# Moving the common first instructions of two programs ahead of the branch that chooses between them

## The chip, the cores and the metric

The kernel runs on the 8 cores of one Trainium2 chip. Each core has five engines with their own instruction streams: PE (TensorE, matrix products), DVE (VectorE), ACT (ScalarE), POOL (GpSimd) and SP (SyncE, here only a queue that starts transfers). Transfers between HBM and the on-chip memory (SBUF) are started by ACT, POOL and SP and carried out by the core's 16 DMA engines. There is no traffic between cores. The metric is the device time of the slowest core in microseconds (us).

## What is computed

One layer of a streaming encoder, on 4 new streams of 4096 frames and on 32 running streams of 64 frames:

```
hn = rms_norm(x, norm1_g)
g_b, g_c, x_a, x_l, g_l = split(hn @ w_in)          # 1024 -> 2560 columns
out_a = g_b * conv3_causal(g_c * x_a)               # mixer A, 512 channels
out_b = rg_lru(conv4_causal(x_l) + b) * gelu(g_l)   # mixer B, a recurrence in time
x = x + concat([out_a, out_b]) @ w_out
x = x + square(relu(rms_norm(x, norm2_g) @ w_up)) @ w_down    # 1024 -> 4096 -> 1024
y = rms_norm(x, norm_f_g)
```

Outputs are y for both groups of streams and the new states of the two convolutions and of the recurrence.

## The kernel before

Two cores share a new stream. The even core does its first 2304 frames, the odd core the remaining 1792. The recurrence runs over the whole stream, so the odd core first recomputes, for the frames of its neighbour, what the state of the recurrence needs (tiles named L). Every core also does 4 running streams (256 rows, tile S). Even cores therefore run the chain of tiles S, M0, M1, M2, M3, M4, and odd cores L0, S, L1 to L4, M0 to M3. An M tile has 512 or 384 rows, an L tile 512 or 256.

The two chains are two programs in one binary. `arm(False)` and `arm(True)` record, for each engine, a list of instructions with their semaphore waits; `emit` (L148) writes both. On every engine the emitted code first reads the word `side` from HBM into a register (L162, two instructions of the form TENSOR_LOAD), then branches (L163): value 0 runs the first program, which stands right behind the branch, and otherwise the second, which stands behind the whole of the first (`make`, L159). Everything else, the first transfer included, stands behind this branch.

What happens first in either program is the work of four strands, generators that yield one instruction at a time:

- `g_par` loads the parameters `par` through ACT's queue and derives small constants in `sb_der` on DVE and ACT;
- `g_xloads` loads rows of x into the 8 slots of 128x1024 f32 (512 KB each) of `sb_xsl`, through ACT's queue. For S and M tiles one transfer fills one slot (`xs` and `xp`); for L tiles, whose input `xl` is stored transposed, one transfer fills two slots (1 MB);
- `g_setup` clears or sets small tiles on POOL (`sb_identb`, ones in `sb_gfb`, `sb_cst`, `sb_halx`, `sb_halp`, `sb_h_p`);
- `g_conv` starts the casting transfers of the weights through POOL's queue: 512 KB of f32 in HBM (`wall`, one chunk of 84) become 256 KB of bf16. The 20 chunks of `w_in` land in SBUF (`sb_ring`, then `sb_uT`), used from there by S, the L tiles and M0, and are written back to `wscr` in HBM through SP (`g_back`) for the later tiles. The other 64 chunks go from HBM to HBM, and SP loads them from `wscr` into a ring when they are needed. `wbd` (the gates' weights) and `wout` are cast by POOL too.

`Weaver` sets the order. It keeps an estimated clock for each engine and each path of transfers, and always emits the waiting instruction with the earliest estimated start. So the position of an instruction in its engine's stream depends on the estimates of all that was emitted before it, and an engine runs its stream in that order, whatever is ready.

PE needs for the first tile: rows in `sb_xsl`, their squares on ACT (`sb_junk`), a scaled copy on DVE (`sb_hb`), transposes on PE (L697), the gain on DVE (into `sb_hT` or, for M0 of the even cores, `sb_uS`), and then the projections with the cast chunks (L776; with the ring, L780). L855 are the gates, L989 is the output projection, L1037 and L1087 are the MLP.

## Time and profile before

| | |
|---|---|
| runs shown | 998.66 us median of 3 (908.91 to 1062.85) |
| profiled execution | 909.05 us, span of its slowest core 907.5 us |
| spans, even cores 0, 2, 4, 6 | 904.6, 903.0, 905.1, 907.5 us |
| spans, odd cores 1, 3, 5, 7 | 901.6, 901.8, 899.8, 902.1 us |
| PE busy on core 6 | 839.3 us (92%) |
| DVE, ACT, POOL busy on core 6 | 425.2, 376.3, 184.9 us |
| moved by core 6 | 158.26 MB |

All times in the profile count from the first instruction of the core in question. "Busy" is the time in which an engine executed something. A row of the timeline gives start, duration, engine, line, operation and names; an engine's name with a q behind it is its instruction sequencer, which is where transfers are started and registers loaded.

### The profile page before, as it was taken

To read this page: it belongs to the slowest core of one execution; us is meant where nothing else is said; L and a number is where in the kernel's file an instruction comes from. 1 tells how busy PE (TensorE), PEld (TensorE's weight loads), DVE (VectorE), ACT (ScalarE), POOL (GpSimd) and SP (SyncE) were. 2 spreads that over 40 slices of the span, in tenths; PEclk is the share of its full clock that TensorE was granted. 3 is DMA by queue.
4 is the path that set the end of the run, shared out by engine and by line. 5 is a ranking of instruction groups with operands and counts; after the bars stand their busy time and mean duration, and the time that the engine had idled before them with its cause. 6 is when DMAs were issued, how large, how long until landed. Compare 5 with 4: busy or idle time off the path is not lost.

```text
span 907.5 us, 15041 instructions; the slowest of 8 cores (899.8 to 907.5 us)
## 1 busy us (share of the span) xinstructions
PE 839.3 (92%) x4392; PEld 428.5 (47%) x4464; DVE 425.2 (47%) x722; ACT 376.3 (41%) x754; POOL 184.9 (20%) x307
## 2 busy tenths in 40 slices
PE   2679789699999999999999999999999899999995
PEld 2444345255564444444444444555445455446542
DVE  4698886663301210636665434575315477514112
ACT  4578738552331000554942134583205485205301
POOL 4132240234453000232100013120003212003200
PEclk9799889899999999999999999999999999999998
DMA  8999999999888534685553369565248852778751
GB/s 237 205 180 215 214 117 130 134 180 177 163 182 168 145 96 126 241 318 172 141 149 84 117 164 300 163 166 161 84 151 254 267 159 73 233 198 271 206 163 73
DMA packets 80441, 158.26 MB, mean 174 GB/s; under 512 B 9184, under 2 KB 9312, under 8 KB 80352
## 3 DMA queue, kind: packets, MB, share of 16 engines
q1 hardware_dynamic: 61632, 111.76, 42.4%
q0 software_dynamic: 15264, 33.30, 23.2%
q10 hardware_dynamic: 3456, 12.14, 4.1%
q8 instruction: 40, 0.66, 0.3%
q14 instruction: 49, 0.40, 0.2%
HBM read 165.75 MB, written 32.57 MB: 219 GB/s over the span
## 4 chain that ended last, share of the span: by engine, by line
PE 82%; DMA 8%; DVE 4%; issue 3%; ACT 2%; POOL 0%; POOLq 0%; DVEq 0%; ACTq 0%; SPq 0%
PE ps L1037 28%; PE ps L1087 27%; PE ps L780 12%; PE ps L989 7%; DMA sb_ring<-wscr 4%; PE ps L776 3%; DMA sb_uT<-wall 3%; PE ps L1079 2%; PE ps L697 1%; PE ps L1097 1%; DMA sb_xsl<-xp 1%; PE ps L855 1%; ACT sb_t_rig L532 1%; PE ps L1074 1%; DVE sb_t_xc L882 1%
## 5 line engine op out<-in xcount | busy, mean ns | idle before, releaser
L1037 PE MATMUL ps<-sb_hT,sb_ring 128*128 128x512 bf16 (+2 forms) x1050 | 194.3, 341 | 6.2 <-DVE sb_a_pb L535 4.3
L532 ACT ACTIVATE sb_junk<-sb_xsl 128x1024 bf16<-128x1024 f32 (+1 forms) x59 | 59.6, 1010 | 269.7 <-DVE sb_xsl L535 256.6
L535 POOL TENSOR_TENSOR sb_uT<-sb_rl 128x512 bf16<-128x512 bf16 (+1 forms) x80 | 83.0, 1038 | 418.4 <-ACT sb_stat L532 272.7
L532 ACT ACTIVATE sb_rl<-ps 128x512 bf16<-128x512 f32 (+2 forms) x192 | 98.1, 525 | 142.2 <-PE ps L1037 127.8
L1037 PEld LDWEIGHTS ps<-sb_hT,sb_ring 128*128 128x128 bf16 x1064 | 104.4, 99 | 91.3 <-issue 8.4
L535 DVE TENSOR_TENSOR sb_xsl<-ps,sb_xsl 128x512 f32<-128x512 f32 (+1 forms) x60 | 46.1, 794 | 200.7 <-PE ps L1087 139.9
L1087 PE MATMUL ps<-sb_ring,sb_uT 128*128 128x512 bf16 x576 | 138.5, 379 | 0.8
L1087 PE MATMUL ps<-sb_uS,sb_uT 128*128 128x512 bf16 x423 | 95.7, 379 | 0.5
L1037 PE MATMUL ps<-sb_hT,sb_uS 128*128 128x512 bf16 (+1 forms) x466 | 92.6, 354 | 0.3
L1087 PEld LDWEIGHTS ps<-sb_ring,sb_uT 128*128 128x128 bf16 x592 | 57.6, 98 | 67.8
L780 PE MATMUL ps<-sb_hT,sb_ring 128*128 128x512 bf16 (+1 forms) x369 | 81.8, 367 | 5.0 <-DMA sb_ring<-wscr 4.6
L535 DVE TENSOR_TENSOR sb_uT<-sb_rl 128x512 bf16<-128x512 bf16 (+1 forms) x80 | 34.0, 425 | 102.6 <-ACT sb_rl L532 90.3
L989 PE MATMUL ps<-sb_wout,sb_mix 128*128 128x512 bf16 x314 | 71.2, 379 | 0.3
L1037 PEld LDWEIGHTS ps<-sb_hT,sb_uS 128*128 128x128 bf16 x472 | 46.0, 98 | 42.9
L1087 PEld LDWEIGHTS ps<-sb_uS,sb_uT 128*128 128x128 bf16 x432 | 42.1, 98 | 49.0 <-issue 0.2
L780 PEld LDWEIGHTS ps<-sb_hT,sb_ring 128*128 128x128 bf16 x376 | 37.1, 99 | 43.4 <-issue 8.4
L532 ACT ACTIVATE sb_t_rig<-sb_t_rig 128x512 f32<-128x512 f32 (+4 forms) x72 | 48.3, 680 | 20.6 <-DVE sb_t_rig L543 19.9
L535 DVE TENSOR_TENSOR sb_hT<-ps,sb_par 128x1024 bf16<-128x1024 bf16 x36 | 43.8, 1220 | 24.7 <-PE ps L697 24.5
L780 PE MATMUL ps<-sb_hT,sb_uS 128*128 128x384 bf16 (+1 forms) x262 | 53.1, 347 | 0.6 <-DVE sb_t_xb L548 0.5
L543 DVE SCALAR_TENSOR_TENSOR sb_t_xc<-sb_t_xb,sb_par,sb_t_xc 128x512 f32<-128x512 f32 (+2 forms) x72 | 46.4, 657 | 13.3 <-ACT sb_t_xc L532 12.1
L532 ACT ACTIVATE sb_t_rig<-sb_t_rig,sb_cst 128x1536 f32<-128x1536 f32 (+5 forms) x48 | 48.2, 1009 | 2.1 <-POOL sb_t_rig L551 0.3
L989 PEld LDWEIGHTS ps<-sb_wout,sb_mix 128*128 128x128 bf16 x320 | 31.2, 98 | 37.5 <-issue 0.7
(100 smaller groups left out, 841.7 us busy)
## 6 DMA issues: line engine op xcount, KB each, us to landing
sb_ring<-wscr SPq DMA_DIRECT2D x240, 256.0 KB, 3.5
sb_uS<-wscr SPq DMA_DIRECT2D x160, 256.0 KB, 3.0
wscr<-wall POOLq DMA_DIRECT2D x64, 256.0 KB, 10.8
sb_xsl<-xp ACTq DMA_DIRECT2D x18, 512.0 KB, 8.7
yp<-sb_xsl POOLq DMA_DIRECT2D x13, 512.0 KB, 7.9
sb_uT<-wall POOLq DMA_DIRECT2D x16, 256.0 KB, 24.1
wscr<-sb_uT SPq DMA_DIRECT2D x16, 256.0 KB, 14.4
sb_wout<-wout POOLq DMA_DIRECT2D x4, 512.0 KB, 13.1
```

Of the source, the lines that this page charges most:

```text
L532: return OP("act", dur, lambda e: e.activation(out=out, in_=in_, func=func, **kw), rd_, wr_)
L535: return OP(eng, dur, lambda e: e.tensor_tensor(out=out, in0=in0, in1=in1, op=op), rd_, wr_)
L543: return OP("dve", dur, lambda e: e.scalar_tensor_tensor(out=out, in0=in0, scalar=scalar, in1=in1, op0=op0, op1=op1), rd_, wr_)
L697: yield PE(0.55, [lambda e, kc=kc: e.transpose(out=pb[:, kc * 128:(kc + 1) * 128], in_=hb_ap[:, kc * 128:(kc + 1) * 128], identity=identb[ ...
L776: lambda e, kc=kc: e.matmul(out=bank_ap(b, N), lhsT=ap[:, kc * 128:(kc + 1) * 128], rhs=h_ap(t, False, kc, col0, N), start=(kc == 0), stop ...
L780: lambda e, kc=kc: e.matmul(out=bank_ap(b, N), lhsT=slot[:, kc * 128:(kc + 1) * 128], rhs=h_ap(t, False, kc, col0, N), start=(kc == 0), st ...
L855: yield PE(0.25, [lambda e, gi=gi, b=b: e.matmul(out=bank_ap(b, N), lhsT=wbd[:, (gi * 4 + c) * 128:(gi * 4 + c + 1) * 128], rhs=T["xcb"][: ...
L882: yield OP("dve", 1.35, lambda e: e.tensor_tensor_scan(out=h, data0=a, data1=i_, initial=h0_p[:, c:c + 1], op0=ALU.mult, op1=ALU.add), [T[ ...
L989: yield PE(4 * 0.217, [lambda e, kc=kc, half=half, b=b, j=j: e.matmul(out=bank_ap(b), lhsT=mix[:, kc * 512 + j * 128:kc * 512 + (j + 1) * ...
L1037: return lambda slot: [lambda e, kc=kc: e.matmul(out=bank_ap(b, q.N), lhsT=slot[:, kc * 128:(kc + 1) * 128], rhs=h_ap(q, True, kc, 0, q.N) ...
L1079: yield PE(32 * 0.217, [lambda e, kc=kc, j=j, bs=bs: e.matmul(out=bank_ap(bs[j]), lhsT=u_ap(t, kc, j * 128, 128), rhs=held[kc // 2][:, (kc ...
L1087: lambda e, i=i, q=q, j=j, b=b: e.matmul(out=bank_ap(b), lhsT=u_ap(q, 2 * kp + i, j * 128, 128), rhs=slot[:, i * 512:(i + 1) * 512], start ...
```

## The change

The inputs are laid out anew on the host: a new array `head` of 128 x 6144 f32 (3 MB) holds what six slots of `sb_xsl` hold at the start, for even cores the two blocks of S and the four of M0, for odd cores the first 2 MB of L0 and the two blocks of S. The array `xs` is gone. The strand `g_head` loads it in four transfers (2, 2, 1 and 1 slots) and fixes which slots belong to which tile; `g_xloads` goes on with the third tile of the chain.

`Weaver.lead` emits a given number of instructions of a strand at once, without choosing by the clock. Each arm first emits: 1 of `g_par` (the transfer of `par`), 4 of `g_head`, 4 of `g_conv` (the casts of chunks 12 to 15), 8 of `g_setup` and 1 more of `g_conv` (the cast of `wbd`). These are the same instructions in both arms, so `emit` writes them once, ahead of the register load and the branch; `cut` is how many each engine has (5 on ACT, 13 on POOL, none on PE, DVE and SP). The rest of each program follows as before, with the order found by the clock from that state on. What is computed does not change.

```
-def emit(nc, arms, side):
+def emit(nc, arms, cut, side):
...
     def make(name):
         def f(e):
+            n = cut[name]
+            put(e, arms[0].prog[name][:n])
             r = e.alloc_register("side")
             e.reg_load(r, side[0:1, 0:1])
             with e.If_eq(r, 0):
-                put(e, name, arms[0])
+                put(e, arms[0].prog[name][n:])
             with e.Else():
-                put(e, name, arms[1])
+                put(e, arms[1].prog[name][n:])
...
+    def lead(self, gen, n):
+
+        s, val = Strand(gen, -99, 0), None
+        pace, self.PACE = self.PACE, {}
+        while n:
+            s.req, val = gen.send(val), None
+            if s.req[0] == "get":
+                val = s.req[1].take(s.req[2])
+            else:
+                self._emit(s, self._start(s.req))
+                n -= 1
+        self.PACE = pace
...
-        Ss = mk_tile("S", "S", xs, 0, 256, 4, 1.5, ys, 0)
+        Ss = mk_tile("S", "S", head, 0, 256, 4, 1.5, ys, 0)
...
+        def g_head():
+            for k, n in ((0, 2), (2, 2), (4, 1), (5, 1)):
+                yield DMA("act", xsl[:, k * D:(k + n) * D], head[:, k * D:(k + n) * D], [], [xsl_b[k + i] for i in range(n)], "x", 0.52 * n)
+            for k in range(6):
+                P_x.free.remove(k)
+            if second_half:
+                Ls[0].xs, Ss.xs = {0: [0, 1], 1: [2, 3]}, {0: 4, 1: 5}
+            else:
+                Ss.xs, Ms[0].xs = {0: 0, 1: 1}, {0: 2, 1: 3, 2: 4, 3: 5}
+            for t in chain[:2]:
+                for _ in t.xs:
+                    W.mark("x" + t.name)
+
         def g_xloads():
-            for t in chain:
+            for t in chain[2:]:
...
-        W.spawn(g_setup(), -20)
-        W.spawn(g_conv(order), 500)
-        W.spawn(g_par(), -19)
-        W.spawn(g_xloads(), -10)
+        setup, conv, pars, rows = g_setup(), g_conv(order), g_par(), g_head()
+        for gen, n in ((pars, 1), (rows, 4), (conv, 4), (setup, 8), (conv, 1)):
+            W.lead(gen, n)
+        cut = {e: len(S.prog[e]) for e in S.ENG}
+        for gen, prio in ((setup, -20), (conv, 500), (pars, -19), (rows, -11), (g_xloads(), -10)):
+            W.spawn(gen, prio)
...
+    tall = lambda a: a.reshape(-1, 128, D).transpose(1, 0, 2).reshape(128, -1)
...
-            "xs": f(x_sample[4 * c:4 * c + 4].reshape(256, D)),
+            "head": f(np.concatenate([wide[:, :4096], few] if hf else [few, tall(rows[:512])], axis=1)),
```

How the streams stand now is shown at three places, all in the program of the even cores or ahead of the branch. In the changed file the lines of the helpers have moved down by 16 (L532 is L548, L551 is L567) and those of the mixer by 30 (L776 is L806); L162 and L163 are L165 and L166.

The start of ACT's stream, before:

```order
L171 UNCONDITIONAL_BRANCH
L162 TENSOR_LOAD side_ptr
L162 TENSOR_LOAD side
L163 COMPARE_AND_BRANCH
L112 DMA sb_par<-par 128x156
L112 DMA sb_xsl<-xs 128x1024 x2
L112 DMA sb_xsl<-xp 128x1024 x6
L532 ACTIVATE sb_der<-sb_der 128x4 x3
L112 DMA sb_gfb<-gf 128x1024
L532 ACTIVATE sb_junk,sb_stat<-sb_xsl 128x1024
```

and in the changed kernel:

```order
L174 UNCONDITIONAL_BRANCH
L112 DMA sb_par<-par 128x156
L112 DMA sb_xsl<-head 128x2048 x2
L112 DMA sb_xsl<-head 128x1024 x2
L165 TENSOR_LOAD side_ptr
L165 TENSOR_LOAD side
L166 COMPARE_AND_BRANCH
L112 DMA sb_xsl<-xp 128x1024 x2
L548 ACTIVATE sb_der<-sb_der 128x4 x3
L112 DMA sb_gfb<-gf 128x1024
L548 ACTIVATE sb_junk,sb_stat<-sb_xsl 128x1024
```

Five transfers (78 KB and 3 MB) stand ahead of the register load; the two behind it are the first of M1.

The start of POOL's stream, before:

```order
L162 TENSOR_LOAD side_ptr
L162 TENSOR_LOAD side
L163 COMPARE_AND_BRANCH
L551 MEMSET sb_identb 128x128
L112 DMA sb_ring<-wall 128x1024
L588 AFFINE_SELECT sb_identb<-sb_identb 128x128
L551 MEMSET sb_gfb 128x128
L551 MEMSET sb_cst 128x1
L112 DMA sb_ring<-wall 128x1024
L551 MEMSET sb_cst 128x1
L551 MEMSET sb_halx 128x12
L551 MEMSET sb_halp 128x8
```

and in the changed kernel:

```order
L112 DMA sb_ring<-wall 128x1024 x4
L567 MEMSET sb_identb 128x128
L604 AFFINE_SELECT sb_identb<-sb_identb 128x128
L567 MEMSET sb_gfb 128x128
L567 MEMSET sb_cst 128x1 x2
L567 MEMSET sb_halx 128x12
L567 MEMSET sb_halp 128x8
L567 MEMSET sb_h_p 128x4
L112 DMA sb_wbd<-wbd 128x1024
L165 TENSOR_LOAD side_ptr
L165 TENSOR_LOAD side
L166 COMPARE_AND_BRANCH
```

The four casts of chunks 12 to 15 are first of all, the cast of `wbd` follows the eight small instructions, and the casts into `sb_uT` come right behind the branch.

PE's first work in the program of the even cores, before:

```order
L697 MATMUL ps<-sb_identb,sb_hb 128x128 x24
L776 MATMUL ps<-sb_hT,sb_ring 128x256 x24
L697 MATMUL ps<-sb_identb,sb_hb 128x128 x16
L776 MATMUL ps<-sb_hT,sb_uT 128x256 x24
L855 MATMUL ps<-sb_t_xcb,sb_wbd 128x256 x4
L776 MATMUL ps<-sb_hT,sb_uT 128x256 x8
L855 MATMUL ps<-sb_t_xcb,sb_wbd 128x256 x2
```

and in the changed kernel:

```order
L727 MATMUL ps<-sb_identb,sb_hb 128x128 x24
L806 MATMUL ps<-sb_hT,sb_ring 128x256 x24
L806 MATMUL ps<-sb_hT,sb_uT 128x256 x8
L727 MATMUL ps<-sb_identb,sb_hb 128x128 x16
L806 MATMUL ps<-sb_hT,sb_uT 128x256 x16
L885 MATMUL ps<-sb_t_xcb,sb_wbd 128x256
L806 MATMUL ps<-sb_hT,sb_uT 128x256 x8
```

One projection of S with the first chunk in `sb_uT` (8 products) now stands ahead of two transposed blocks of M0, and one pair of gates is split. Such exchanges go on through the even program's first three tiles and through the whole L part of the odd one.

## Rows read from the trace of the kernel before

**Rows 1.** Spans and mean TensorE clock of the cores.

```profile
core 0: 904.6 us, clock 0.979
...
core 5: 899.8 us, clock 0.950
core 6: 907.5 us, clock 0.976
core 7: 902.1 us, clock 0.946
```

**Rows 2.** Busy time of each engine by stretch, core 6.

```profile
core 6: us, PE busy (x) PEld busy (x) DVE busy (x) ACT busy (x) POOL busy (x), PEclk, DMA share, GB/s
20.00:60.00 40.00, 25.82 (x185) 18.51 (x185) 29.31 (x71) 24.82 (x61) 9.84 (x23) 0.84 1.04 200
60.00:180.00 120.00, 99.47 (x501) 48.78 (x509) 92.33 (x163) 80.57 (x138) 30.77 (x60) 0.91 0.99 164
180.00:300.00 120.00, 118.90 (x655) 64.47 (x667) 38.01 (x59) 39.49 (x82) 49.57 (x77) 1.00 0.94 178
```

**Rows 3.** Chain that ended last, core 6: start, duration, what.

```profile
1.02 0.90 POOLq L162
1.95 0.52 POOLq L162
...
7.64 26.93 DMA sb_uT<-wall
...
144.09 13.34 DMA sb_ring<-wscr
```

**Rows 4.** Timeline of core 6, start of ACT, POOL and PE.

```profile
2.58 0.38 ACTq L112 DMA_DIRECT2D sb_par<-par  x1
3.16 0.72 POOL L112 DMA_DIRECT2D sb_ring<-wall  x1 [0.34 <-POOL sb_identb L551]
3.95 3.94 ACTq L112 DMA_DIRECT2D sb_xsl<-xp  x6
6.60 3.20 POOL L112 DMA_DIRECT2D sb_uT<-wall  x6
10.69 1.06 ACT L532 ACTIVATE sb_junk<-sb_xsl 128x1024 bf16<-128x1024 f32 x1 [0.30 <-POOL sb_a_pb L548]
30.44 1.87 PE L776 MATMUL ps<-sb_hT,sb_uT 128*128 128x256 bf16 x8 [4.91 <-DMA sb_uT<-wall]
```

**Rows 5.** Transfers of core 6: KB each, median us from issue to landing.

```profile
sb_xsl<-xs ACTq DMA_DIRECT2D x1, 512.0 KB, 4.3
sb_xsl<-xs ACTq DMA_DIRECT2D x2, 512.0 KB, 5.4
```

**Rows 6.** Timeline of core 7, start of POOL, ACT and DVE.

```profile
5.50 0.20 POOL L551 MEMSET sb_identb<- 128x128 bf16 x1 [4.79 <-issue]
9.44 0.72 POOL L112 DMA_DIRECT2D sb_ring<-wall  x1 [3.73 <-issue]
9.94 1.11 ACTq L112 DMA_DIRECT2D sb_xsl<-xl  x2
20.38 2.28 DVE L539 TENSOR_SCALAR sb_hT<-sb_xsl,sb_par 128x512 bf16<-128x512 f32 x4 [1.49 <-DMA sb_xsl<-xl]
```

**Rows 7.** Queue: packets, MB, engine share; core 6, 8 to 12 and 20 to 24 us.

```profile
q10 hardware_dynamic: 234, 0.83, 54.8%
q0 software_dynamic: 222, 0.39, 51.8%
...
q0 software_dynamic: 171, 0.32, 51.4%
q10 hardware_dynamic: 175, 0.65, 51.2%
```

**Rows 8.** Transfers of core 7 from 10 to 12 us, then 12 to 16 us.

```profile
DMA packets 30, 0.02 MB, mean 9 GB/s; under 512 B 0, under 2 KB 30, under 8 KB 30
...
DMA packets 321, 0.83 MB, mean 208 GB/s; under 512 B 32, under 2 KB 130, under 8 KB 259
```

More of the change, by code:

```diff
@@ L143, in check_no_deadlock, with put @@
             raise RuntimeError("static deadlock: " + "; ".join(msg))
-def emit(nc, arms, side):
-    def put(e, name, S):
-        for waits, fns, inc in S.prog[name]:
+def emit(nc, arms, cut, side):
+    def put(e, part):
+        sem = arms[0].sem
+        for waits, fns, inc in part:
             for k, v in waits:
-                e.wait_ge(S.sem[k], v)
+                e.wait_ge(sem[k], v)
             ins = None
@@ L156, in put @@
             if inc is not None:
-                ins.then_inc(S.sem[inc[0]], inc[1])
+                ins.then_inc(sem[inc[0]], inc[1])
     def make(name):
         def f(e):
+            n = cut[name]
+            put(e, arms[0].prog[name][:n])
             r = e.alloc_register("side")
@@ L381, in dout @@
         return nc.dram_tensor(name, list(shape), dt, kind="ExternalOutput").ap()
-    xp, xl, xs = din("xp", [NF, D]), din("xl", [128, 8 * NF]), din("xs", [256, D])
+    xp, xl, head = din("xp", [NF, D]), din("xl", [128, 8 * NF]), din("head", [128, 6 * D])
     side_d = din("side", [1, 1], mybir.dt.int32)
@@ L645, in arm @@
         chain = Ls[0:1] + [Ss] + Ls[1:] + Ms
+        assert [t.J if not t.lean else 4 for t in chain[:2]] in ([4, 2], [2, 4])
         def xap(k):
@@ L1188, in arm @@
         S.check_no_deadlock()
-        return S, W
+        return S, W, cut
     with es:
         arms = [arm(False), arm(True)]
-        emit(nc, [a[0] for a in arms], side_d)
+        emit(nc, [a[0] for a in arms], arms[0][2], side_d)
+        assert arms[0][2] == arms[1][2]
     return nc, arms[0][1], arms[1][1]
@@ L1225 @@
         rows[:len(mine)] = mine
+        wide = f(np.concatenate([x_prompt[s, a:a + n].reshape(n, 8, 128).transpose(2, 1, 0).reshape(128, 8 * n)
+                                 for a, n in zip(np.cumsum((0,) + SKIP), SKIP)], axis=1))
+        few = tall(x_sample[4 * c:4 * c + 4].reshape(256, D))
         st = np.concatenate([sca[4 * c:4 * c + 4].reshape(8, 512), slc[4 * c:4 * c + 4].reshape(12, 512), slh[4 * c:4 * c + 4]], axis=0)
@@ L1230 @@
             "xp": rows,
-            "xl": f(np.concatenate([x_prompt[s, a:a + n].reshape(n, 8, 128).transpose(2, 1, 0).reshape(128, 8 * n)
-                                    for a, n in zip(np.cumsum((0,) + SKIP), SKIP)], axis=1)),
-            "xs": f(x_sample[4 * c:4 * c + 4].reshape(256, D)),
+            "xl": wide,
+            "head": f(np.concatenate([wide[:, :4096], few] if hf else [few, tall(rows[:512])], axis=1)),
             "side": np.full((1, 1), hf, np.int32),
```

## Prediction

> **What bounds the kernel now.** I read the spans first. The metric is the slowest core, and that is an even core: core 6 ends at 907.5 us, core 0 at 904.6; the odd cores shown end at 899.8 and 902.1 [rows 1]. A gain on odd cores alone is worth nothing, and a loss there costs nothing before it exceeds 907.5 - 902.1 = 5.4 us. The profiled execution took 909.05 us, 1.5 more than its longest span; my sum is made against it. The median of the three runs shown, 998.66, is far above it and their lowest, 908.91, is beside it; I forecast the time of an execution like the profiled one.
>
> Next, the busy times by stretch on core 6 [rows 2]. From 180 to 300 us PE is busy 118.90 of 120: from there on the end is fixed by PE's own work. From 20 to 60 it is busy 25.82 of 40 and from 60 to 180 99.47 of 120, while the DMA engines' share is 1.04 and 0.99. So the core is short of transfers there, and what the change does to the end is how much earlier or later the stream of transfers, and PE behind it, gets through the first 180 us.
>
> The chain agrees [rows 3]: after two register loads (1.02 to 2.47 us) and a few starts on POOL it is 26.93 us of a casting transfer into `sb_uT`; much later a load of the ring (13.34 us from 144.09) is in it. PE's first wait for such a cast ends at 30.44, after 4.91 us of idling [rows 4]. Not ACT, not DVE, but bytes in a full pipe decide when the S tile gets on.
>
> **The start of the even cores.** ACT issues its first transfer at 2.58 and POOL its first cast at 3.16, behind the 1.5 us of register loads and branch [rows 3, 4]. With nothing ahead of them both can go at about 1.05, where the first load now starts: 1.5 us earlier on ACT, 2.1 on POOL. Both feed the same 16 engines, so I take 1.8.
>
> What stands behind must not fall dry. ACT: 0.4 for `par`, two transfers of two slots at 0.55 each (a pair took 1.11 on core 7 [rows 6]), two of one slot at up to 0.66 (3.94 for six [rows 4]), which ends at about 3.9; loads and branch 1.5, to 5.4; the two transfers of M1 1.3, to 6.7. Before, the last of the eight was issued at 3.95 + 3.94 = 7.9, so ACT's arithmetic can start 1.2 earlier. POOL: four casts (0.72, then 0.53 each, from 3.20 for six [rows 4]) to 3.4, the eight small instructions beside and behind them, `wbd` to about 4.2, loads and branch to 5.7, and the first cast into `sb_uT` there instead of at 6.60. These casts queue: in the chain one takes over 26 us from issue to landing, so the 0.9 matters as little as the 1.5 us of branch that now sits between the two groups. Price of a dry queue: those 1.5 us once; the 5.5 MB issued ahead cover it (below).
>
> On even cores the first transfer now brings both blocks of S. Before, they were issued right behind `par`, at about 3.0 and 3.5; block 0 took 4.3 to land and the median of the two is 5.4, so block 1 took 6.5: they landed at 7.3 and 10.0 [rows 5]; ACT squared the first from 10.69 on [rows 4], held by the derivation of the constants. Now both land together near 10.0 - 1.5 = 8.5, ACT is ready at about 9.5. So the coarser transfer costs nothing; without that cover it would be 10.0 - 7.3 = 2.7 us on the first square, and still ahead of the 4.91 us that PE waits for a cast.
>
> **The neighbour.** This is the term that decides. Core 7 has to run the second program, and issues its first cast at 9.44 and its first rows at 9.94 [rows 6]. From 10 to 12 us it moves 9 GB/s, from 12 to 16 208 GB/s [rows 8]. So before 12 us core 6 streams alone. What is that worth? In 8 to 12 us core 6 served 234 packets of ACT's queue in 54.8% of 16 x 4 us, 0.150 us each, and 222 of POOL's in 51.8%, 0.149 each. In 20 to 24 us, with core 7 streaming, 175 took 51.2%, 0.187 each, and 171 took 51.4%, 0.192 each [rows 7]. Packets have the same mean size (3.5 to 3.7 KB, 1.8 to 1.9 KB). With the neighbour, a packet takes 1.27 times as long.
>
> After the change the odd cores start at the same time as the even ones, since the shared head needs no branch. The 8.4 us of lone streaming (3.6 to 12 us) are gone: the same packets take 8.4 x 0.27 = 2.3 us longer. From 12 to 20 us the neighbour was still coming up; if half of the rise was missing there, another 0.7 at most. So the even cores lose 2.3 to 3.0 and gain 1.8: +0.5 to +1.2 us, of which I take +0.8. Bounds: if the dearer packet has another cause (later packets differ, SP's write-backs), the loss is 0 and the sum -1.8; if all of 12 to 20 us was cheap too, it is 16.4 x 0.27 = 4.4, and the sum +2.6.
>
> The Trainium skill, HBM Reference, Specifications, says that the two cores of a domain share its bandwidth, each getting about 358 GB/s with both streaming. By that a core at 305 GB/s (core 6 from 8 to 12 us: 1.22 MB in 4 us) would lose nothing to its neighbour, and the time would come out at the -1.8 of the first rival; core 6's own packets speak against it here.
>
> **The odd cores.** First rows at about 1.5 instead of 9.94: 8.4 us earlier, so the first cast into `sb_hT` (20.38 [rows 6]) could come at 12. At most that takes core 7 from 902.1 to 893.7; the new L orders may eat some. It does not show in the metric.
>
> **The new order.** It moves no work. One projection of S with a chunk of `sb_uT` now stands ahead of 16 transposes of M0, which will wait for that chunk; M0's products come long after, so I cost it at nothing. If such an exchange goes wrong where nothing covers it, the nearest row is PE's wait for one cast, 4.91 us [rows 4]; exchanged luckily it may give as much. PE's idle time in 60 to 180 us, 20.5 us [rows 2], is what can be won at all.
>
> **Sum.** 909.05 - 1.8 + 2.6 = 909.8 us.
>
> **Rivals.**
> Rival 1, the neighbour costs nothing. For: HBM may not be the reason of the dearer packet. Against: all of it falls together with core 7's start. Then 909.05 - 1.8 = 907.3 us.
> Rival 2, the order wins: an exchange takes away one wait like the 4.91. For: PE has 20.5 us of idle time there. Against: nothing says which way it goes. 909.8 - 4.9 = 904.9 us.
> Rival 3, slower: an exchange puts PE behind a cast or a DVE result that it did not wait for, with later work queued behind it. Same price, 909.8 + 4.9 = 914.7 us; it decides once the blocked work is needed before 60 us, where PE still idles a third of the time.
> Rival 4, slower by code. The odd cores' second program is not at hand after the branch: POOL idles 4.79 us until 5.50 and 3.73 more until 9.44 [rows 6], with nothing else in flight. Now 3 MB of rows and 2.5 MB of weights are queued; at the 0.97 MB in 4 us of the later pair in rows 7 they fill 22 us. If the code comes behind all of it, core 7 starts at 22 + 6.9 (9.44 - 2.55) + about 2 = 31 instead of 20.38, ends at 912.7, and the run is 914.2 us. It decides when that first cast comes after 20.38 + 5.4 = 25.8. Against: code has a queue of its own. The Trainium skill, Runtime: NRT & Kernel Launch, Instruction fetch mechanics, says that a taken branch out of the window forces a transfer of the target page first; the trace agrees with the two idle times, and the page says nothing of what data does to them.
>
> **How the numbers follow.** Forecast, 909.8 (own range 907.5 to 912.5): 0.45. Rival 1: 0.2. Rival 2: 0.15. Rival 3: 0.12. Rival 4: 0.08. The range takes in rivals 1 and 2 with 0.3% of scatter (2.7 us) below rival 2 and as much above rival 3: 902 to 917.5. Only several such exchanges, or a fetch that waits twice, leave the 2% (18 us) that a measurement of this kernel tells from no change: slower 0.04, faster 0.03, same 0.93.
>
> **What the profile of the changed kernel would show.** First issues of ACT and POOL at about 1.05 on all cores; first branch on ACT ending near 5.4, on POOL near 5.7. Core 6's packets at 0.19 rather than 0.15 us in 8 to 12 us, and no more than 250 GB/s there. PE's first wait for a cast ending between 29 and 32. Core 7's first cast into `sb_hT` near 12 and its span under 900. Even cores still the slowest, within 3 us of before. Packets at 0.15 us and core 6 near 905.7 would speak for rival 1, a core 7 above core 6 for rival 4, equal transfers with another PE idle time in 60 to 180 us for rivals 2 and 3.

## The result and the profile after

The changed kernel takes 912.28 us in the median (910.63 to 915.83) where the one before takes 910.31; the ratio is 1.0032, 95% interval 1.0024 to 1.0041, so +2.9 us. The forecast was +0.8. Four of the 19 executions before ran 10 to 17% longer at a lower clock on some cores; such executions are left out of every ratio and mean below, and the median of the other 15 is 909.51. The profiled execution of the changed kernel took 914.98 us, 2.7 above its median, and the one before 909.05, 0.5 below 909.51: so the two traces differ by more than the kernels do (5.9 us against 2.9), and the readings below show the kind of loss and not its exact size. These are its spans and clocks; beside [rows 1], the even cores are later and the odd ones earlier:

```profile
core 0: 910.4 us, clock 0.978
...
core 2: 913.4 us, clock 0.976
...
core 5: 898.5 us, clock 0.944
core 6: 910.1 us, clock 0.978
core 7: 900.8 us, clock 0.944
```

The mean over all its executions is 909.3 on the even cores and 898.1 on the odd ones; with the kernel before it was 904.1 to 906.1 and 899.5 to 902.1 on the five chips on which the experiments ran. The clocks are those of [rows 1] to within 0.006.

Where did the time arise? Start with the timeline of core 6, changed kernel, ACT, POOL and PE (start, duration; in brackets the engine's idle time ahead of the row), beside [rows 4]:

```profile
1.07 0.38 ACTq L112 DMA_DIRECT2D sb_par<-par  x1
1.59 2.33 POOL L112 DMA_DIRECT2D sb_ring<-wall  x4 [0.88 <-POOLq L391]
10.98 1.05 ACTq L112 DMA_DIRECT2D sb_xsl<-xp  x2
12.07 1.06 POOL L112 DMA_DIRECT2D sb_uT<-wall  x2 [6.06 <-issue]
14.80 1.06 ACT L548 ACTIVATE sb_junk<-sb_xsl 128x1024 bf16<-128x1024 f32 x1 [0.30 <-issue]
34.25 1.87 PE L806 MATMUL ps<-sb_hT,sb_uT 128*128 128x256 bf16 x8 [6.36 <-DMA sb_uT<-wall]
```

Both queues start 1.5 us earlier, as meant. Then nothing is issued from 3.8 to 10.98 on ACT. The next view, the instructions of the register load on core 6 (duration in ns, min/median/max, then the start in us), shows why:

```profile
L165 SPq TENSOR_LOAD <-side_ptr x1: 860/860/860, 1.1 to 1.1; - x1
...
L165 ACTq TENSOR_LOAD <-side_ptr x1: 5886/5886/5886, 3.8 to 3.8; - x1
L165 POOLq TENSOR_LOAD <-side_ptr x1: 5184/5184/5184, 5.4 to 5.4; - x1
L165 ACTq TENSOR_LOAD <-side x1: 1144/1144/1144, 9.7 to 9.7; - x1
L165 POOLq TENSOR_LOAD <-side x1: 844/844/844, 10.7 to 10.7; - x1
```

SP reads its word from HBM while nothing streams, in 0.86 us. ACT and POOL read theirs behind their own 3 MB and take 5.9 and 5.2 us for the first of the two loads; I had put 1.5 us for both loads and the branch. The first square comes 4.1 us later than before, the first cast into `sb_uT` 5.5. Core 6 is the mildest case: on cores 0, 2 and 4 ACT's two loads take 8.9, 7.9 and 8.3 us, and the first square comes 6.3 to 6.5 us later than before.

The transfers of core 6, by queue in 8 to 12 us, answer to [rows 7]:

```profile
DMA packets 202, 1.00 MB, mean 250 GB/s; under 512 B 10, under 2 KB 10, under 8 KB 103
...
q10 hardware_dynamic: 101, 0.81, 69.8%
q0 software_dynamic: 101, 0.19, 30.6%
```

ACT's packets are now twice as large (8 KB), so I compare by bytes: 0.81 MB in 69.8% of 16 x 4 us is 55 us per MB; before it was 0.83 MB in 54.8%, 42. That is 1.30 times, and 250 GB/s is the bound that the prediction named. POOL's packets have the size of before (1.8 to 1.9 KB) and take 0.194 us (30.6% of 64 us, 101 packets) instead of 0.149, as forecast. By stretch (columns as in [rows 2]), core 6, first before the change, then changed:

```profile
0.00:4.00 4.00, 0.00 (x0) 0.00 (x0) 0.00 (x0) 0.00 (x0) 1.23 (x7) 1.00 0.07 17
4.00:8.00 4.00, 0.00 (x0) 0.00 (x0) 0.79 (x4) 0.02 (x1) 4.00 (x14) 1.00 0.97 252
8.00:12.00 4.00, 0.00 (x0) 0.00 (x0) 1.19 (x6) 3.04 (x7) 3.89 (x11) 1.00 1.07 306
12.00:16.00 4.00, 1.16 (x10) 0.95 (x11) 2.14 (x5) 3.47 (x10) 0.00 (x0) 1.00 1.05 313
16.00:20.00 4.00, 2.61 (x20) 1.94 (x19) 3.79 (x5) 2.18 (x6) 0.00 (x0) 1.00 1.07 285
```

```profile
0.00:4.00 4.00, 0.00 (x0) 0.00 (x0) 0.00 (x1) 0.00 (x0) 2.62 (x9) 1.00 0.49 98
4.00:8.00 4.00, 0.00 (x0) 0.00 (x0) 0.79 (x4) 0.00 (x0) 1.38 (x9) 1.00 0.97 238
8.00:12.00 4.00, 0.00 (x0) 0.00 (x0) 0.00 (x0) 0.00 (x0) 0.00 (x0) 1.00 1.00 250
12.00:16.00 4.00, 0.00 (x0) 0.00 (x0) 1.04 (x7) 3.05 (x6) 3.93 (x11) 1.00 1.04 219
16.00:20.00 4.00, 1.36 (x14) 1.39 (x15) 2.11 (x5) 3.72 (x10) 1.34 (x3) 1.00 1.00 222
```

The last column times 4 us is the bytes. The earlier start brings 0.32 MB in the first 4 us; the next 16 us lose 0.91 MB, and in 12 to 20 us the loss per us is the largest. At 20 us core 6 has moved 4.11 instead of 4.69 MB; over the four even cores the mean is 3.98 instead of 4.75. At the 250 GB/s that both cores of a pair then get, 0.77 MB is 3.1 us. Part of that is made up at once: from 20 to 24 us core 6 runs at 321 GB/s, where it had 247. PE's wait for its first cast into `sb_uT` ends at 34.25 instead of 30.44 (34.50, 35.35 and 36.53 on cores 4, 2 and 0). The first product of the down projection starts at 282.1 on the mean of the even cores instead of 276.1 (278.4 in e_order and 277.7 in n_before, two kernels of the table below). From 180 to 300 us PE is busy for 120.00 of 120 us.

The chain on core 6 has the same kind of casting transfer as [rows 3], 7 us later:

```profile
14.68 29.71 DMA sb_uT<-wall
```

Core 7, beside [rows 6], starts at once and then stalls; its casts into `sb_uT` and its first write of L0 into `sb_hT` come late (the other odd cores write `sb_hT` from 23.96, 24.36 and 25.00):

```profile
1.48 3.26 ACTq L112 DMA_DIRECT2D sb_xsl<-head  x4
...
20.86 3.70 POOL L112 DMA_DIRECT2D sb_uT<-wall  x7 [14.86 <-issue]
...
26.19 4.65 DVE L555 TENSOR_SCALAR sb_hT<-sb_xsl,sb_par 128x512 bf16<-128x512 f32 x8
```

Where the 14.86 us of idling went is told by POOL's loads and branch on core 7, the branch of the kernel before first, then the changed kernel:

```profile
L163 POOLq COMPARE_BRANCH  x1: 45/45/45, 2.4 to 2.4; - x1
```

```profile
L165 POOLq TENSOR_LOAD <-side_ptr x1: 4440/4440/4440, 5.4 to 5.4; - x1
L165 POOLq TENSOR_LOAD <-side x1: 3994/3994/3994, 9.9 to 9.9; - x1
L166 POOLq COMPARE_BRANCH  x1: 45/45/45, 13.9 to 13.9; - x1
```

The two loads take 8.4 us. From the branch to POOL's first cast behind it are 7.0 us (13.9 to 20.86), and before the change they were 7.0 as well (2.4 to 9.44).

### The profile page after: what moved, and what is told of

Read it like the earlier page. It is cut to its first block, busy times and chain, and to the rows that moved or that the text cites. A ratio compares the mean times of both kernels' runs of the same rounds, so it can differ in the third digit from the quotient of the medians.

```text
span 913.4 us, 15044 instructions; the slowest of 8 cores (895.5 to 913.4 us)
## 1 busy us (share of the span) xinstructions
PE 839.4 (92%) x4392; PEld 429.8 (47%) x4464; DVE 426.6 (47%) x718; ACT 376.4 (41%) x754; POOL 182.1 (20%) x307
## 4 chain that ended last, share of the span: by engine, by line
PE 82%; DMA 7%; issue 4%; DVE 3%; ACT 2%; POOLq 1%; POOL 0%; DVEq 0%; ACTq 0%; SPq 0%
PE ps L1067 27%; PE ps L1117 27%; PE ps L810 12%; PE ps L1019 7%; PE ps L806 4%; DMA sb_ring<-wscr 4%; DMA sb_uT<-wall 2%; PE ps L727 2%; PE ps L1109 2%; PE ps L1127 1%; DMA sb_xsl<-xp 1%; PE ps L885 1%; PE ps L1104 1%; DVE sb_t_xc L559 1%; ACT sb_t_rig L548 1%
## 5 line engine op out<-in xcount | busy, mean ns | idle before, releaser
L1067 PE MATMUL ps<-sb_hT,sb_ring 128*128 128x512 bf16 (+2 forms) x1048 | 194.4, 340 | 10.3 <-DMA sb_ring<-wscr 8.7
L548 ACT ACTIVATE sb_junk<-sb_xsl 128x1024 bf16<-128x1024 f32 (+1 forms) x59 | 59.5, 1009 | 270.8 <-DVE sb_xsl L551 265.5
L551 POOL TENSOR_TENSOR sb_uT<-sb_rl 128x512 bf16<-128x512 bf16 (+1 forms) x80 | 81.5, 1018 | 414.4 <-ACT sb_stat L548 272.3
L548 ACT ACTIVATE sb_rl<-ps 128x512 bf16<-128x512 f32 (+2 forms) x192 | 97.8, 524 | 145.9 <-PE ps L1067 134.4
L551 DVE TENSOR_TENSOR sb_xsl<-ps,sb_xsl 128x512 f32<-128x512 f32 (+1 forms) x56 | 45.5, 839 | 200.8 <-PE ps L1117 140.7
L551 DVE TENSOR_TENSOR sb_uT<-sb_rl 128x512 bf16<-128x512 bf16 (+1 forms) x80 | 34.2, 428 | 102.2 <-ACT sb_rl L548 95.0
L551 DVE TENSOR_TENSOR sb_hT<-ps,sb_par 128x1024 bf16<-128x1024 bf16 x36 | 43.9, 1220 | 30.7 <-PE ps L727 30.3
L548 ACT ACTIVATE sb_t_rig<-sb_t_rig 128x512 f32<-128x512 f32 (+4 forms) x72 | 48.4, 680 | 12.5 <-DVE sb_t_rig L559 10.5
L727 PE MATMUL ps<-sb_identb,sb_hb 128*128 128x128 bf16 x320 | 27.6, 242 | 27.3 <-DVE sb_hb L555 24.9
L548 ACT ACTIVATE sb_t_rig<-sb_t_rig,sb_cst 128x1536 f32<-128x1536 f32 (+5 forms) x48 | 48.3, 1012 | 2.3 <-POOL sb_t_rig L567 0.3
## 6 DMA issues: line engine op xcount, KB each, us to landing
wscr<-wall POOLq DMA_DIRECT2D x64, 256.0 KB, 10.5
```

The lines of the kernel that those rows point to most:

```text
L548: return OP("act", dur, lambda e: e.activation(out=out, in_=in_, func=func, **kw), rd_, wr_)
L551: return OP(eng, dur, lambda e: e.tensor_tensor(out=out, in0=in0, in1=in1, op=op), rd_, wr_)
L727: yield PE(0.55, [lambda e, kc=kc: e.transpose(out=pb[:, kc * 128:(kc + 1) * 128], in_=hb_ap[:, kc * 128:(kc + 1) * 128], identity=identb[ ...
L1067: return lambda slot: [lambda e, kc=kc: e.matmul(out=bank_ap(b, q.N), lhsT=slot[:, kc * 128:(kc + 1) * 128], rhs=h_ap(q, True, kc, 0, q.N) ...
```

## Experiments

The table gives each kernel's ratio and, since the slowest core is nearly always an even one unless the odd ones are held back, the mean span of the even and of the odd cores over the executions of the ratio, less that of the kernel before on the same chip, with twice the standard error. The second column is the start in us of core 7's first transfer of rows in the profiled execution (9.9 in the kernel before; the other odd cores lie up to 4 us beside it, in e_odd_late7 7 to 10 us behind it).

| kernel | odd rows from | ratio, 95% | even, us | odd, us |
|---|---|---|---|---|
| n_before | 10.5 | 1.0010 (1.0000 to 1.0021) | +0.5 ± 0.6 | -0.1 ± 1.0 |
| b_place | 9.1 | 1.0014 (1.0001 to 1.0026) | +0.4 ± 0.6 | +0.1 ± 0.9 |
| e_head | 10.4 | 1.0018 (1.0009 to 1.0028) | +1.3 ± 0.5 | +1.7 ± 0.6 |
| e_head_rows | 9.8 | 1.0014 (0.9999 to 1.0030) | +1.0 ± 0.7 | +2.5 ± 0.7 |
| e_order | 9.8 | 1.0008 (1.0000 to 1.0017) | +0.8 ± 0.7 | -0.5 ± 1.2 |
| e_order_rows | 9.0 | 1.0030 (1.0019 to 1.0041) | +1.7 ± 0.5 | +3.1 ± 0.6 |
| e_oldorder | 1.5 | 1.0031 (1.0015 to 1.0048) | +2.3 ± 0.7 | -5.9 ± 1.6 |
| e_oldorder_rows | 1.5 | 1.0037 (1.0021 to 1.0052) | +3.1 ± 0.8 | +0.3 ± 1.2 |
| e_regfirst | 2.8 | 1.0039 (1.0022 to 1.0055) | +2.9 ± 0.9 | -11.2 ± 0.7 |
| e_old_regfirst | 2.8 | 1.0048 (1.0034 to 1.0062) | +3.8 ± 0.8 | -8.1 ± 0.9 |
| a_rows | 1.5 | 1.0029 (1.0017 to 1.0042) | +2.6 ± 0.5 | -0.4 ± 0.9 |
| e_odd_one | 4.4 | 1.0035 (1.0022 to 1.0047) | +3.2 ± 0.6 | -3.2 ± 1.1 |
| b_odd_one | 13.2 | 1.0003 (0.9993 to 1.0013) | 0.0 ± 0.6 | +1.2 ± 0.9 |
| e_odd_late2 | 16.9 | 1.0050 (1.0032 to 1.0067) | -1.1 ± 1.2 | +10.3 ± 0.9 |
| b_odd_two | 19.2 | 1.0027 (1.0015 to 1.0038) | -0.6 ± 1.1 | +5.9 ± 0.9 |
| e_pairs | 3.1 (core 5), 38.4 (core 7) | 1.0242 (1.0214 to 1.0270) | +3.1 ± 1.3 (0, 4), -0.5 ± 1.1 (2, 6) | -6.5 (1, 5), +27.8 (3, 7) |
| b_odd_late4 | 37.2 | 1.0169 (1.0147 to 1.0190) | -3.7 ± 1.0 | +20.9 ± 0.9 |
| e_odd_late7 | 36.6 | 1.0268 (1.0242 to 1.0294) | -1.4 ± 0.9 | +29.4 ± 1.1 |

### What the comparison itself shows for no change

n_before is the kernel before, unchanged.

> The kernel before itself, unchanged, run as if it were a changed kernel: what this comparison shows for no change. If the +0.8 to +1.7 us of the four kernels with `head` and nothing hoisted are a bias of the comparison, this shows it too: even cores about +1.2. If they belong to the kernels: even and odd cores within 0.5 us (twice the standard error of such a difference was 0.5 to 0.7), ratio 1.000.

It came out at 1.0010 and +0.5 us on the even cores. So differences of 0.5 us on the even cores, and 0.9 on the slowest, are not told from nothing here, and the changed kernel's 1.0032 may hold some 0.9 us of this. Everything below is read against that floor.

### Everything but the earlier start

e_order is the changed kernel with `n = 0` in `make`: the array, the large transfers and the new order are there, but nothing stands ahead of the branch.

> The changed kernel with nothing ahead of the branch: new array, new order of both programs, start as before. Theory A (the two register loads, which take 9 us behind the queued rows, are the cost): no loss is left, ratio to before 0.999 to 1.001, core 6 near 908. Theory B (the new order costs: SP has 15 write-backs instead of 10 ahead of the first load of the ring, PE waits for it): the loss stays, ratio 1.003 to 1.006, first product from the ring on even cores near 120 us instead of 109, first L1087-type product (down projection) 4 to 8 us later than before. Theory C (the neighbour's early traffic): odd cores start late again, so like A.

1.0008, +0.8 us on the even cores: most of the loss appears only when instructions are moved ahead of the branch (1.0032 - 1.0008 = 0.0024 or 2.2 us, each against the kernel before of its own set). PE's first projection starts at 17.8 us (19.3 before).

e_head has the old order and six transfers of 512 KB, but out of `head`:

```
-                    yield DMA("act", xap(k), t.src[t.row0 + j * 128:t.row0 + (j + 1) * 128, :], [], [xsl_b[k]], "x", 0.52)
+                    if t in chain[:2]:
+                        src = head[:, k * D:(k + 1) * D]
...
+                    yield DMA("act", xap(k), src, [], [xsl_b[k]], "x", 0.52)
```

> Edit: e_oldorder with nothing taken out of the branches, so the only difference from the kernel before is the array `head`, whose 128 rows are 24 KB apart where two rows of the old arrays were 4 KB apart. Theory 1 (the neighbour's early traffic is the whole loss): nothing starts earlier on any core, so even and odd cores stay within 0.5 us of the kernel before, ratio 1.000 (0.999 to 1.001). Rival (the array's spread rows cost time themselves, as a comparison of b_odd_late4's even cores, 901.3, with e_odd_late7's, 903.6, would allow): even cores 1 to 2 us later, ratio 1.001 to 1.002.

+1.3 us, which looked like a price of the layout. (Its odd cores also load L0's first 2 MB in four transfers of 512 KB instead of two of 1 MB; they are at +1.7.) Four further kernels tested that. In the three with `_rows` the array is `din("head", [6 * 128, D])`, read as `head[k * 128:(k + 1) * 128, :]`; b_place only makes `xs` 2 MB longer.

> Edit: e_head, with `head` stored as 768 rows of 4 KB, one behind the other, as the old arrays were, instead of 128 rows of 24 KB; same bytes, same transfers. Theory P (the 1.3 us that e_head's even cores lost come from the spread of the addresses: a tile's 128 rows lie 24 KB apart): even cores back within 0.4 us of before, ratio 1.000 (0.999 to 1.001), and core 0 moves 260 GB/s again in 4 to 8 us where e_head moved 227. Theory Q (another array at another place, whatever its shape, or chance): even cores 1 to 1.5 us later again, ratio 1.0015 to 1.002.

> Edit: e_order (new order and `head`, nothing taken out of the branches), with `head` stored as 768 rows of 4 KB. e_order was at +0.7 us on even cores, e_head (old order, `head`) at +1.3, so the new order by itself should be -0.6. Theory P: even cores 0.6 us (0 to 1) ahead of the kernel before, ratio 0.999 to 1.000. Theory Q: +0.7 as e_order, ratio 1.001.

> Edit: the changed kernel, with `head` stored as 768 rows of 4 KB; the transfers of two slots read two blocks of 128 such rows. Theory P: even cores 1.3 us earlier than in the changed kernel (+3.1 to +3.5 over before there), so at +1.8 to +2.2, ratio 1.002; what is left is the neighbour less the earlier start. Theory Q: as the changed kernel, 1.0032. Rival R (the neighbour alone is the whole loss and e_head's was chance): 1.003 or more, with e_head_rows at 1.000.

> The kernel before, with the array `xs` made 2 MB longer (it carries the first 512 rows of the prompt as well, which nothing reads from there), so that it has the size of `head` and shifts what lies behind it by the same 2 MB; every transfer reads the same rows in the same order as before. If the +1.2 us of the kernels with `head` come from where the arrays lie in memory: even cores +1 us, odd cores +1.5 to +2.5, ratio 1.001. If they come from reading the first prompt rows out of the same array as the samples, or from the doubled number of separate first transfers on the odd cores: within 0.5 us of before, ratio 1.000.

Theory P falls: with rows of 4 KB the even cores are at +1.0, +1.7 and, with the head hoisted, +2.6. The placement falls too (+0.4). What stays: the four kernels with `head` and nothing hoisted are at +0.8, +1.7, +1.3 and +1.0, 1.2 on the mean, where n_before and b_place are at +0.5 and +0.4. So some 0.7 ± 0.5 us come with `head` or the order of its transfers. Two kernels with late odd cores, on one chip and both in the old order, point the same way: e_odd_late7, with `head`, has its even cores at -1.4 ± 0.9, b_odd_late4, without it, at -3.7 ± 1.0. On what they rest stays open: neither the rows' distance nor the array's place, and no view of the traces shows a place for it (e_head_rows has moved as many bytes by 20 us as before: 239 against 241 GB/s on core 0, 234 against 235 on core 6). These kernels, not the one before, are the right zero for what follows.

### The earlier start and the neighbour, one by one

e_oldorder is e_head with the first 7 instructions of ACT and 13 of POOL ahead of the branch. e_old_regfirst is the same but reads the register before them, so that the even cores start when they did before, and only the odd ones earlier:

```
         def f(e):
             n = cut[name]
-            put(e, arms[0].prog[name][:n])
             r = e.alloc_register("side")
             e.reg_load(r, side[0:1, 0:1])
+            put(e, arms[0].prog[name][:n])
             with e.If_eq(r, 0):
```

> The order of before on every engine and in both programs, six transfers of 512 KB from the new array, and the common first part (7 instructions of ACT, 13 of POOL) ahead of register load and branch. Theory A: register loads again take about 9 us under traffic, ratio 1.003 or more. Theory B: no loss, ratio at or under 1.000, first product from the ring near 109 + what the start costs. Theory C: ratio 1.002 to 1.003 with packets of 0.19 us in 8 to 12 us.

> As e_oldorder, but the register loads come first and the common part behind them. Even cores then start at 2.5 as before, in the same order as before; only the odd cores' transfers start 7 us earlier. Theories A and B: ratio 1.000, odd cores 2 to 8 us shorter. Theory C: whatever loss there is beyond 1.000 is the neighbour's; my estimate was 2.3 to 3.0 us, ratio 1.0025 to 1.0033.

The even cores' own earlier start, with the slower register loads behind it, is worth 2.3 - 3.8 = -1.5 ± 1.1 us (same chip). The odd cores' start, 7 us earlier, costs +3.8 over before, and 3.8 - 1.3 = 2.5 ± 1.0 over e_head (two chips). Core 6 of e_old_regfirst, by stretch, against the five rows of before above:

```profile
4.00:8.00 4.00, 0.00 (x0) 0.00 (x0) 0.70 (x4) 0.00 (x0) 4.00 (x14) 1.00 1.00 163
8.00:12.00 4.00, 0.00 (x0) 0.00 (x0) 0.17 (x1) 1.80 (x4) 3.79 (x11) 1.00 1.02 207
12.00:16.00 4.00, 0.00 (x0) 0.00 (x0) 1.92 (x8) 2.96 (x8) 0.00 (x0) 1.00 1.07 221
16.00:20.00 4.00, 1.32 (x12) 1.11 (x13) 1.21 (x2) 1.53 (x4) 0.00 (x0) 1.00 0.99 251
```

POOL is as busy as before and the engines' share is full, but the bytes fall from 252, 306, 313 and 285 GB/s to these: by 1.55, 1.48, 1.42 and 1.14. That is 1.26 MB by 20 us, 5 us at 250 GB/s; about half of it, 2.5, reaches the end. Part is made up: on the mean of the even cores 1.26 MB are missing at 20 us and 0.95 at 60.

e_regfirst is the changed kernel with the register load put first in the same way.

> The changed kernel with the register loads first, then the common part, then the branch. The loads should take 0.9 and 0.5 us again, and the first transfers start at about 2.5 on all cores, on even cores as before. Theory A: the loss goes, ratio 0.999 to 1.001; first square on ACT near 10.7 instead of 14.8. Theory B: ratio 1.003 or more, whatever the start. Theory C (odd cores now stream from 2.5 us on): 1.002 to 1.003.

1.0039 against 1.0032 for the changed kernel, and 2.9 - 0.8 = +2.1 ± 1.1 us over e_order for the neighbour alone. With the loads in front again and the first square on core 6 at 10.87 the even cores are no faster. This kernel takes away two things together, the slow register loads (5.9 + 1.1 us) with the late square, and the 1.5 us of earlier start, so what is shown is that the two nearly balance; what either costs alone is not shown. The DMA engines did not fall dry meanwhile: in the changed kernel their share is 1.00 from 8 to 12 us, although nothing is started until 10.98. That is the prediction's cover (5.5 MB in the queues) at work, longer than I had asked of it. The odd cores gain 11 us: core 7 issues its casts into `sb_uT` from 14.68 instead of 20.86.

### One kernel, two pairs early and two late

In e_pairs (e_old_regfirst, with 14 further register loads on cores 3 and 7 ahead of the head) cores 0 and 4 have an early neighbour and cores 2 and 6 a late one, in the same executions.

```
+                r2 = e.alloc_register("idle")
+                with e.If_eq(r, 2):
+                    for _ in range(14):
+                        e.reg_load(r2, side[0:1, 0:1])
...
-            "side": np.full((1, 1), hf, np.int32),
+            "side": np.full((1, 1), 2 if c in (3, 7) else hf, np.int32),
```

> As e_old_regfirst (order of before, register loads first, common part behind them), but on cores 3 and 7 fourteen more register loads stand ahead of the common part and hold their transfers back by about 7 us; cores 1 and 5 start at 2.5. If the loss comes from the neighbour of the pair: cores 0 and 4 show packets of 0.20 to 0.30 us in 4 to 12 us and reach their down projection at 281 to 285 us as in e_old_regfirst, cores 2 and 6 show 0.15 us and reach it at 274 to 279 as before, and end 3 to 6 us ahead of 0 and 4. If it comes from all eight cores starting at once: the four even cores are alike and between the two.

```profile
core 0: 909.4 us, clock 0.975
...
core 2: 903.6 us, clock 0.980
...
core 4: 907.7 us, clock 0.979
...
core 6: 902.9 us, clock 0.979
```

Cores 0 and 4 are at +3.2 and +3.0 over the kernel before, cores 2 and 6 at -0.6 and -0.5 (means over executions). No floor of a comparison enters the 3.6 ± 1.7 us between the pairs. The same queues tell it; q10 and q0 in 8 to 12 us, first core 0, then core 2:

```profile
q10 hardware_dynamic: 169, 0.62, 59.9%
q0 software_dynamic: 144, 0.27, 42.6%
```

```profile
q10 hardware_dynamic: 234, 0.83, 55.1%
q0 software_dynamic: 219, 0.39, 51.7%
```

A packet of q10 takes 0.227 us (59.9% of 64 us, 169 packets) and one of q0 0.189 beside a streaming neighbour, 0.151 each alone. So the cost goes by the partner of the pair and not by the rest of the chip: this is shown. (The 3.6 us are between a neighbour at 3 us and one at 38, so they also hold what a late neighbour gives.)

### How the cost goes with the neighbour's start

The other kernels shift the odd cores by register loads on ACT and POOL, ahead of the common head (e_odd_...: `If_eq(r, 1)` and 1, 4 or 14 loads as in e_pairs), or at the start of their branch in the kernel before (b_odd_...: 1, 2 or 8).

> Edit: e_odd_late2 with one register load instead of four on ACT and POOL of each odd core ahead of its common part. The odd cores were 7 us earlier than before in e_old_regfirst and 10 us later with four loads; one load should put their first transfer between 3 us earlier and 1 us later than before, some 3 us behind the even cores. Theory A (the loss grows in proportion to the early start): even cores between 0 and 1.7 us over the kernel before (3.8 x 3/7), ratio 1.000 to 1.002. Theory B (what costs is that both cores of a pair stream in the very same 4 us, packets there 0.26 to 0.34 us against 0.16 to 0.18): with 3 us between them the even cores are at +0.5 or less, ratio 1.000. Theory C (any start of the odd core ahead of the old one costs the full 3.8 us): even cores over +3, ratio 1.004.

> Edit: the kernel before, with one further register load on ACT and POOL at the head of the odd cores' branch, so that the odd cores start 1 to 5 us later; nothing else. If the pair shares memory as the runs so far say, the even cores gain: 8 loads (28 us) gave them 3.7 us, 7 us of earlier start cost 3.8, so 1 to 5 us should give 0.3 to 1.5 us on the even cores and cost the odd ones 0.5 to 4: slowest core about 905 to 906 mean, ratio 0.9985 to 0.9995. Rival (what the even cores lost in the changed kernel is tied to its first 8 us alone, and nothing is to be had beyond the old start): even cores within 0.3 us, ratio 1.000.

> The same with two register loads: the odd cores start 3 to 8 us later. Sharing: even cores 1 to 2 us faster, odd ones at 903 to 906, ratio 0.9975 to 0.9995, the best of this row if the even cores' gain still outruns the odd cores' loss. Rival: even cores within 0.3 us of before and the odd ones 3 to 6 later, still not the slowest: ratio 1.000.

> The same with four register loads, about 2 us. If the loss is plain sharing of bandwidth, it shrinks in proportion to the lone time: ratio about 1.0035. If it comes from two cores in step (the same addresses asked for at the same moment), 2 us break most of it: 1.001 or less.

> The kernel before, with eight register loads ahead of the odd program on ACT and POOL, so that the odd cores start 4 us later still (rows at about 13.8). If the neighbour's start sets the even cores' time: they gain another 1 to 2.5 us, ratio 0.997 to 0.999, odd cores at 904 to 906. If not: 1.000.

> The same kernel with all four odd cores held back by fourteen register loads, about 7 us. Code, order and start of the even cores are those of e_old_regfirst. If only the time at which the neighbour starts matters: ratio 1.000 (0.999 to 1.001), first projection on core 6 near 19.3 again instead of 24.1. If the place of the code or the new array costs: 1.003 to 1.005 stays.

I had put 0.5 us for a load, and they took far longer. Core 3 of b_odd_late4, the added loads on ACT (POOL's are alike):

```profile
L168 ACTq TENSOR_LOAD <-side_ptr x8: 980/2854/4852, 5.6 to 37.5; - x8
...
L168 ACTq TENSOR_LOAD <-side x8: 579/1203/2472, 10.5 to 38.6; - x8
```

So the shifts are those of the table's second column, not those of the expectations. Read in its order, the even cores' cost falls as the neighbour comes later, but not in proportion: +3.8 at 2.8 us and still +3.2 at 4.4, where theory B of e_odd_one (only the very same 4 us count) wanted under 0.5 and theory A (in proportion) at most 1.7, while theory C's "over +3" is met; then 0.0 at 13.2, -0.6 at 19.2 and -3.7 at 37.2, with the array of before. No such shift beats the kernel before: b_odd_one is at 1.0003 with n_before at 1.0010, and from two loads on the odd cores are the slowest. Core 6 of b_odd_late4 shows what is being shared: from 16 to 24 us it runs at 324 and 315 GB/s, where before it had 285 and 247:

```profile
16.00:20.00 4.00, 1.97 (x16) 1.46 (x16) 3.01 (x4) 1.96 (x6) 0.00 (x0) 1.00 1.06 324
20.00:24.00 4.00, 3.86 (x21) 2.80 (x22) 2.06 (x3) 2.33 (x6) 0.72 (x2) 1.00 1.09 315
```

e_oldorder_rows was to give start and neighbour alone against the recorded +0.8.

> Edit: e_oldorder (old order, 7 instructions of ACT and 13 of POOL ahead of the branches), with `head` stored as 768 rows of 4 KB: the earlier start and the neighbour alone, with neither the array's spread nor the new order. My recorded terms are -1.8 for the start and +2.6 for the neighbour, +0.8 in all. Theory P: e_oldorder's +2.3 less e_head's 1.3, so +1.0 on even cores, ratio 1.001: the recorded terms hold and the layout is what they lacked. Theory Q or R: +2.3 again, ratio 1.0025 to 1.003: the neighbour's term was mis-sized.

+3.1 ± 0.8 on the even cores, beside +1.0 ± 0.7 of e_head_rows on the same chip. Start and neighbour together are thus 3.1 - 1.0 = 2.1 ± 1.1; the same difference is 1.0 for e_oldorder and e_head (two chips) and 0.9 for a_rows and e_order_rows. Their mean is 1.3 with some ± 0.6, against the recorded 0.8. The changed kernel less e_order, which can be had as ratios only, gives 2.2; with it, and the other three as ratios too (2.1, 1.2 and -0.1), the mean is again 1.3. So start and neighbour together came out near the recorded sum, and none of these differences by itself is sharp enough to tell 0.8 from 1.3.

## Why the prediction was right and wrong

- **Bound by bytes, even cores decide, odd cores don't: right.** The slowest core is even in all 19 executions of the changed kernel. The odd cores' changes from -11 to +3 us hardly showed in the ratio: an odd core was the slowest in 2 of 10 executions of e_order_rows and 4 of 11 of b_odd_one.
- **The neighbour, taken as +2.6: right in the end, by two errors that cancel.** Against the right zeros it is +2.5 ± 1.0 (e_old_regfirst less e_head, on two chips), +2.1 ± 1.1 (e_regfirst less e_order) and +1.8 ± 0.8 (e_odd_one less e_head). Rival 1 is false: a cost of 0 lies outside all three. But the bytes that went missing were twice those of my working. The factor 1.27 came from 20 to 24 us; at the start of both streams it is 1.55, 1.48 and 1.42. And for 12 to 20 us I allowed half of the rise, where before the change packets in 12 to 16 us were as cheap as alone, 0.157 and 0.153 us (core 6, q0 and q10):

```profile
q0 software_dynamic: 184, 0.34, 45.1%
q10 hardware_dynamic: 185, 0.69, 44.3%
```

  There was a slip too: half of a rise of 0.27 over 8 us is 1.1 us and not the 0.7 of the prediction. The working gave 2.3 us, with the half rise 3.0, or 0.6 to 0.75 MB at 250 GB/s; measured were 1.26 MB. I had also taken a missing byte to cost its full time at the end, and about half of it did.
- **The start, -1.8: over-sized, the first of two steps that failed.** First issues came at 1.07 and 1.59 as written, but they gave 1.5 ± 1.1 us (e_oldorder less e_old_regfirst) and, by the ratios, 0.6 us between the changed kernel and e_regfirst: about 1, so 0.8 too much. In both comparisons the early start brings the slow register loads with it. Whether the start itself is worth less than 1.8, or the loads take some of it back, stays open.
- **The new order and the array, costed at nothing: the second step that failed.** 0.7 ± 0.5 us come with them; which of the two it is, and by what path, stays open. Of the new order the prediction says "It moves no work" and "I cost it at nothing"; that the rows come from another array got no term at all. Rivals 2 and 3, an exchange worth 4.9 us, have no part in it: e_order has the new order and the array without the earlier start and is at +0.8.
- **Register loads and branch behind the head, 1.5 us: wrong.** 7.1 us on ACT, 6.1 on POOL of core 6. What they cost by themselves is not told from what the earlier start gives: e_regfirst, without either, shows the same time.
- **PE's first wait for a cast to end between 29 and 32: wrong,** 34.25 to 36.53 on the four even cores. The missing bytes and the casts issued 5.5 us later (core 6) both point that way; their shares were not separated.
- **Core 7's first cast into `sb_hT` near 12: wrong,** 26.19, beyond even the 25.8 from which rival 4 should decide: casts into `sb_uT` only at 20.86 after 14.86 us of idling. But it was not the code: from POOL's branch to its first cast are 7.0 us as before, and on the four odd cores, ACT and POOL, 6.4 to 7.5 in the changed kernel against 6.9 to 8.0. What made it late are the register loads, 8.4 us where I had 1.5, and the 7.0 us behind the branch, which I had left out for all that is not in the head. And core 7 ended at 900.8, not at 912.7: a late L0 did not shift the odd core's end by as much. Rival 4 is false in both halves.
- **The sum anew:** neighbour +2.2 (mean of the three; recorded 2.6), start -1 (recorded -1.8), array and order +0.7 (recorded 0): +1.9 in all, where the record has +0.8. Up to 0.9 more is what the unchanged kernel shows on its slowest core when compared in this way, which makes +2.8 beside the measured +2.9. That last term is a property of the comparison and no time of the kernel, and with its interval of 0 to 1.9 us (1.0000 to 1.0021) it may be chance. Each term is uncertain by 0.5 to 1 us, so the split is the best that these runs give and no more, and the close agreement of the sum is partly luck; that the neighbour is the largest term is shown, that the array or order has a part is likely.

The Trainium skill, HBM Reference, Specifications, gives each of two streaming cores about 358 GB/s, by which nothing would have been lost. The trace disagrees: core 6 at 313 GB/s alone falls to 221, and in 8 to 12 us of e_old_regfirst cores 6 and 7 have 207 and 217 GB/s. These figures count a casting transfer by the 256 KB that it writes and not by the 512 KB that it reads; counted by what is read, core 6 has (0.57 + 2 x 0.26) MB in 4 us, 272 GB/s, and still under the page's share. The measurement decides.

## What to carry to other kernels

If two cores share their memory and one of them is ahead of the other in the critical work, an earlier start of the uncritical one is paid by the critical one (here some 2.2 us for 7 us of earlier start): look in several windows, with and without the partner's traffic, and sum the missing bytes up to the point where both are steady. Take the price of contention from the phase in which it will occur, not from the nearest steady one. An edit that is costed at nothing wants a kernel of its own that holds this edit alone, and the unchanged kernel should be run once as if it were a change, before a few tenths of a per cent are given a cause.

## What the hardware showed that I had not expected

- Reading one word from HBM into a register takes 0.9 + 0.5 us on a quiet pair and 5.9 + 1.1 us behind a queue of 3 MB (ACT of core 6; 7.9 to 8.9 us in all on the other even cores). It is slow too when only the other core of the pair streams: on core 3 of b_odd_late4, whose queues were empty, the median was 2.9 + 1.2 us and the longest 4.9 + 2.5.
- The wait for code behind the branch did not grow with the data queued: 6.4 to 7.5 us from branch to first transfer on ACT and POOL of the odd cores with 3 MB and the casts queued, 6.9 to 8.0 before. The kernels that branch earlier, while both cores open their streams, show 7.2 to 8.9 (ACT and POOL of the odd cores in e_old_regfirst).
- Two cores of a pair in the same opening (rows of 4 KB and casting transfers) move 424 GB/s together in 8 to 12 us (207 + 217) and 493 together in 20 to 24 us before (247 + 246); one alone moves 296 to 324 (core 6 of b_odd_late4, 8 to 24 us).
- With larger packets (8 KB, changed kernel) the pair had 250 + 247 GB/s in 8 to 12 us. The time per MB on q10 was 55 us, against 67 in e_old_regfirst (0.57 MB in 60.1%). That the packet size is the reason was not tested by itself.
